# Merge stage: output units as one 512- and one 256-column product, two more copies and sums, another order on ScalarE, and six stores at the end

## The reference, cut to what matters

```python
mixed = (jax.nn.sigmoid(f["g_a"]) * (y_a.astype(dt) @ lp["w_a"])
         + jax.nn.sigmoid(f["g_b"]) * (y_b.astype(dt) @ lp["w_b"]))
return mixed @ lp["w_out"]
...
return _rmsnorm_2(h, final_norm).astype(x.dtype)
```

## Time and profile before

| | |
|---|---|
| median of 3 runs | 2354.12 us (2350.52 to 2354.69) |
| the profiled execution | 2346.09 us |
| its span | 2344.2 us |
| TensorE busy | 2285.3 us, 97% |
| VectorE, ScalarE, GpSimd busy | 1223.2, 1178.7, 1342.1 us |
| merge stage, in the span | about 1000 to 1273 us |
| stores at the end | 4 of 512 KB |

### The profile page before, as it was taken

The page is one execution under the profiler, slowest core; times in us unless marked ns, Lnnn a source line. Parts: engine busy times, 40 slices in busy tenths (PEclk is TensorE's granted clock), DMA queues, the critical chain, the costliest instruction groups (busy, mean ns, idle before and its releaser), DMA issues.

```text
span 2344.2 us, 60261 instructions
## 1 busy us (share of the span) xinstructions
PE 2285.3 (97%) x23364; PEld 1944.4 (83%) x23364; DVE 1223.2 (52%) x2449; ACT 1178.7 (50%) x1999; POOL 1342.1 (57%) x566
## 2 busy tenths in 40 slices
PE   6999999999999999999999999999999999999997
PEld 4787787778777888899999888888888888888886
DVE  2478778877883323466565455453444533333322
ACT  3244545454554444444444555555555555555554
POOL 1112123212332344478888878777777877778785
PEclk8999999999999999999999999999999999999999
DMA  9922112211211223267776555555555555555553
GB/s 389 381 87 66 40 60 77 66 41 58 70 65 50 81 99 108 99 222 251 256 252 244 183 166 176 168 173 173 177 172 171 181 169 172 177 177 172 170 181 134
DMA packets 101244, 360.70 MB, mean 154 GB/s; under 512 B 11184, under 2 KB 14768, under 8 KB 101072
## 3 DMA queue, kind: packets, MB, share of 16 engines
q1 hardware_dynamic: 99872, 356.89, 44.4%
q10 hardware_dynamic: 1200, 1.25, 0.2%
HBM read 356.00 MB, written 2.10 MB: 153 GB/s over the span
## 4 chain that ended last, share of the span: by engine, by line
PE 89%; DVE 2%; ACT 2%; issue 1%; DVEq 0%; ACTq 0%
PE ps L223 32%; PE ps L224 16%; PE ps L684 5%; PE ps L196 4%; PE ps L198 4%; PE ps L197 4%; PE ps L686 4%; PE ps L685 4%; PE ps L815 1%; PE ps L800 1%; PE ps L836 1%; PE ps L980 1%; PE ps L850 1%; PE ps L951 1%; PE ps L1000 1%
## 5 line engine op out<-in xcount | busy, mean ns | idle before, releaser
L187 POOL TENSOR_TENSOR wlo<-raw,whi 128x1024 fp32r<-128x1024 f32 x555 | 1336.7, 2422 | 948.7 <-ACT whi L178 898.7
L223 PE MATMUL ps<-acts,whi 128*128 128x512 f32 x3072 | 1087.6, 398 | 1.3 <-DVE acts L2794 1.3
L224 PE MATMUL ps<-acts,wlo 128*128 128x256 f32 x3072 | 856.7, 279 | 0.0
L178 ACT ACTIVATE whi<-raw 128x1024 fp32r<-128x1024 f32 x562 | 591.6, 1054 | 267.1 <-PE ps L224 138.3
L223 PEld LDWEIGHTS ps<-acts,whi 128*128 128x128 f32 x3072 | 576.2, 188 | 131.6 <-DVE acts L2794 1.6
L224 PEld LDWEIGHTS ps<-acts,wlo 128*128 128x128 f32 x3072 | 579.0, 188 | 0.9
L684 PE MATMUL ps<-acts,whi 128*128 128x512 f32 (+1 forms) x560 | 216.9, 387 | 0.9 <-DVE W L1560 0.9
L686 PE MATMUL ps<-acts,wlo 128*128 128x512 f32 (+1 forms) x560 | 190.1, 339 | 0.0
L685 PE MATMUL ps<-acts,whi 128*128 128x512 f32 (+1 forms) x560 | 189.8, 339 | 0.0
L196 PE MATMUL ps<-acts,whi 128*128 128x256 f32 (+1 forms) x576 | 181.7, 315 | 0.0
L198 PE MATMUL ps<-acts,wlo 128*128 128x256 f32 (+1 forms) x576 | 180.0, 313 | 0.0
(11 more groups left out here) (391 smaller groups left out, 3087.8 us busy)
## 6 DMA issues: line engine op xcount, KB each, us to landing
raw<-stream SPq DMA_DIRECT2D x564, 512.0 KB, 3.3
W<-stream SPq DMA_DIRECT2D x64, 512.0 KB, 9.1
graw<-stream SPq DMA_DIRECT2D x32, 512.0 KB, 4.3
W<-xT SPq DMA_DIRECT2D x4, 1024.0 KB, 8.7
XR<-xT SPq DMA_DIRECT2D x16, 128.0 KB, 5.7
outT<-XR SPq DMA_DIRECT2D x4, 512.0 KB, 3.3
cns<-consts SPq DMA_DIRECT2D x1, 928.0 KB, 11.1
cns<-consts SPq DMA_DIRECT2D x1, 896.0 KB, 7.4
```

Of the source, the lines that this page charges most:

```text
L178: nc.scalar.activation(high, raw[slot], ACT.Copy).then_inc(hi_done, 1)
L187: nc.gpsimd.tensor_tensor(wlo[slot], raw[slot], whi[slot].bitcast(F32), ALU.subtract).then_inc(lo_done, 1)
L223: nc.tensor.matmul(both_parts, whi[slot][:, k, :], hl[:, :, k0 + k, :], start=first and k == 0, stop=False)
L224: ins = nc.tensor.matmul(ps[:, bank, 0:T], wlo[slot][:, k, :], hl[:, 0, k0 + k, :], start=False, stop=last and k == UK - 1)
```

## The change

The output units of a merge tile go through `mm_wide` as well. ScalarE makes two more copies per tile (into `sqv`, free in this stage) and VectorE two more sums, each ahead of the product that reads it. ScalarE's split `hi(k + 7)` moves ahead of the high part of the mixed result. In `out3` the small logarithm that loads the table moves ahead of the last tile's square (for the other output phases its place stays). VectorE's first piece of the last product is cut in two, GpSimd's too, and there are six stores in place of four.

```diff
                     for u in range(2):
                         M["ylo"].wait(pe, (2, 5)[u])
-                        mm_unit(pe, (b + 4 + u) % RING, i * 12 + (b + 4 + u), ps[:, bank + 2 + u, 0:T], 1, UK * u, True,
-                                True)
+                        mm_wide(pe, (b + 4 + u) % RING, i * 12 + (b + 4 + u), bank + 2 + u, acts[:, :, 1], UK * u, True, True)
...
                     hi(k + 5, k + 6)
+                    act.wait_ge(unit_used, i * 12 + (S_MERGE + k + 6))
+                    M["out_sum"].wait(act, i * 4 + 2 * n)
+                    for u in range(2):
+                        parts_copy(act, out_low(u), bank + 2 + u).then_inc(M["out_lo"].sem, 1)
+                    hi(k + 7)
                     M["mix"].wait(act, i * 2 + n + 1)
                     nc.scalar.activation(mhi[:, bass.ds(2 * i + n, 1), :].rearrange("p a t -> p (a t)"), mx[:, n, :],
                                          ACT.Copy).then_inc(M["mhi"].sem, 1)
-                    hi(k + 7)
...
                     for g in range(2):
+                        M["out_lo"].wait(dve, i * 4 + 2 * n + g + 1)
+                        parts_sum(dve, out_low(g), 6 - 4 * n + g).then_inc(M["out_sum"].sem, 1)
+                        M["out_sum"].wait(dve, i * 4 + 2 * n + g + 1)
                         nc.vector.scalar_tensor_tensor(tg[:, n, T * g:T * g + T], tg[:, n, T * g:T * g + T], 1.0,
                                                        ps[:, 6 - 4 * n + g, 0:T], ALU.add, ALU.mult)\
                             .then_inc(M["m1"].sem, 1)
...
                             hi(i, k)
+                        if i == KT // 2 - 1 and k == (4 if base == S_OUT3 else 5):
+                            nc.scalar.activation(small[:, 106:107], kst_[:, 3:4], ACT.Ln if base == S_OUT3 else ACT.Sqrt)
                         if n is not None:
                             tile(i, n)
                         if i == KT // 2 - 1 and k == 5:
-                            nc.scalar.activation(small[:, 106:107], kst_[:, 3:4], ACT.Ln if base == S_OUT3 else ACT.Sqrt)
...
-            for k in range(4, KT, 4):
-                nc.vector.tensor_tensor(XR[:, k:k + 4, :], XR[:, k:k + 4, :],
-                                        ps[:, 7, 0:T].unsqueeze(1).broadcast_to([P, 4, T]), ALU.mult).then_inc(N["x"].sem, 1)
+            for k, n in ((4, 2), (6, 2), (8, 4), (12, 4)):
+                nc.vector.tensor_tensor(XR[:, k:k + n, :], XR[:, k:k + n, :],
+                                        ps[:, 7, 0:T].unsqueeze(1).broadcast_to([P, n, T]), ALU.mult).then_inc(N["x"].sem, 1)
...
-            nc.gpsimd.tensor_tensor(XR[:, 0:4, :], XR[:, 0:4, :], sr[:, T:2 * T].unsqueeze(1).broadcast_to([P, 4, T]),
-                                    ALU.mult).then_inc(N["tab"].sem, 1)
+            for k in (0, 2):
+                nc.gpsimd.tensor_tensor(XR[:, k:k + 2, :], XR[:, k:k + 2, :], sr[:, T:2 * T].unsqueeze(1).broadcast_to([P, 2, T]),
+                                        ALU.mult).then_inc(N["tab"].sem, 1)
...
+            for k, n, ready, value in ((4, 2, "x", 1), (6, 2, "x", 2), (0, 2, "tab", 1), (8, 4, "x", 3), (2, 2, "tab", 2),
+                                       (12, 4, "x", 4)):
+                S["out3"][ready].wait(sp, value)
+                sp.dma_start(outT[:, k:k + n, :], XR[:, k:k + n, :]).then_inc(stored, 16)
+            sp.wait_ge(stored, 96)
```

More of the change, by code:

```diff
@@ L2008, in dve_gla @@
                         .then_inc(G["head_done" if m else "const"].sem, 1)
-        M = counts("m", "yhi ylo x_in c_in tg m1 m2 mix mhi mlo xr gate_in0 gate_in1 gate_acc gate_mm gate_ok gate_lo gate_sum", 1)
+        M = counts("m", "yhi ylo x_in c_in tg m1 m2 mix mhi mlo xr gate_in0 gate_in1 gate_acc gate_mm gate_ok gate_lo gate_sum out_lo out_sum", 1)
         retire(G)
@@ L2045, in gate_low, with out_low @@
             return qk[:, T * g:T * g + T]
+        def out_low(u):
+            return sqv[:, u, 0:T]
         assert M["mix"].base > 1
```

## The result

The changed kernel takes 2380.9 us (median of 6 runs, 2375.8 to 2386.9), the kernel before 2352.6 in the runs beside it: a ratio of 1.0122, 95% interval 1.0109 to 1.0134. It is slower by 28 us. The direction and the place (the merge) were forecast, the size was forecast at 39.

What follows compares the result with a forecast made beforehand. TensorE alone bound the merge before; the change would close a loop of waits of 20.0 us against 17.07 a tile. +41.0, -0.4 in the other two tiles, -1.65 at the end: 2354 + 39 = 2393 us, range 2368 to 2405.

Steps and rivals of the forecast that it cites:

- the loop: Merge: gate products, gate load, unit 3's load and split, copies, sums, mixed result, low part, next gate products; 20.0 us.
- the output copies behind the split of unit 3: Merge, ScalarE: the mixed result waits for copies queued behind a split that waits for DMA, closing the loop.
- Size of a turn: Merge: 5.8 to unit 3's split, 7.8 to the low part's end, 6.4 of gate products: 20.0 us against 17.07.
- When it binds: Merge: slack is used up in the first two tiles, then 14 of 16 run at 20.0 us: +41.0 us.
- The order of the splits: Merge, ScalarE: moving the next split ahead of the high part costs nothing under TensorE, at most 1.06 us in the loop.
- the 7.8: Merge: time in us from the start of unit 3's split to the end of the low part, including holding by GpSimd.
- a loop without holding: Merge: if GpSimd holds none of VectorE's operations, the loop is 17.4 us and the total +3 us.
- Output products: Merge, TensorE: 16 pairs in place of 16 triples save 0.2 us a tile, 3.2 us for 16 tiles.
- The prediction's second sum: Merge, output products: estimate by N/2.4 + 2.5 ns per matmul, 328 against 325 ns, 0.7 us saved in all.
- The end: Output phase: table load ahead of the last square -1.15 us, earlier first store less 0.1 for store costs; -1.65 in all.
- Rivals: Three other merge outcomes: 2349 us (chance 0.14), 2357 us (0.08), 2361 us (0.06).
- The first: Merge: unit 3's load lands in 3.3 us, nothing held, TensorE bounds; gain 4.9 us, time 2349; chance 0.14.

Runs made afterwards that it cites:

- experiment 7: The changed kernel with SyncE's two gate loads one place later in its list, ScalarE's and VectorE's orders kept: ratio to the kernel before 1.0019.
- experiment 4: The changed kernel with the mixed result's high part again ahead of the split of unit 4, copies still behind unit 3's split: ratio to before 1.0023.
- experiment 3: The changed kernel with the two output copies ahead of the splits of units 3 and 4, high part still behind unit 4's: ratio to before 1.0134.
- experiment 2: The kernel before with only ScalarE's split of the next tile's unit 4 moved ahead of the mixed result's high part: ratio to before 1.0120.
- experiment 5: The changed kernel with output copies ahead of the split of unit 3 and high part ahead of the split of unit 4: ratio to before 0.9993.
- experiment 6: The kernel before with the output units as pairs and nothing else, no copies and no sums: ratio to before 1.0005.

## Why the prediction was right, and where it was not

*What bounds, and the loop.* Right in the main. Every link is in the chain of the changed kernel, and shortening the SyncE link (experiment 7) takes away 24 of the 28 us. But the link by which the prediction closes the loop, the output copies behind the split of unit 3, is not the one that matters: with it and without the moved split the loss is 5 us (experiment 4), without it and with the moved split it is 31 (experiment 3).

*Size of a turn, 20.0 against 18.75.* Three terms. From the gate products to the split of unit 3 5.8 was forecast and 5.4 measured, the landing being 4.5 in place of 4.9. From there to the end of the scaling 4.25 was forecast and 4.24 measured, the add held by GpSimd as said. From there to the end of the low part 3.55 was forecast and 2.7 measured: unit 4's load landed 3.0 after unit 3's, not 3.9, so its split was no longer in the high part's way. The prediction had said that an earlier load would leave this sum the same within 0.2; it became 0.8 shorter. Gate products: 6.4 both. Both misses are landing times that were taken from another tile (4.9 and 7.6, here 4.5 and 6.4) with the same loads just ahead in SyncE's list. Why they landed later there was not found; the last older weight load, issued at 1195.5, had landed at 1198.7. 14 x (20.0 - 18.75) = 17.5 us too much, more than the whole miss of 39 against 28: other terms erred the other way.

*When it binds, 14 tiles.* Right: the first turn is 17.2, the next 19.2. 14 turns of 18.96 in place of 17.07 are 26.5 of the merge's 27.3. The turn taken apart above is one of the shorter ones: 14 x 1.68 would be 23.5. What lengthens the others was not separated; in the longest, 19.8, TensorE waits 1.2 for the modulation's gate.

*The order of the splits.* **This step was wrong.** It said that the split ahead costs nothing where TensorE is the bound, and at most 1.06 a tile inside the loop. Experiment 2 shows that it alone makes 1.012, experiment 4 that taking it back recovers 23 us, about 1.7 a tile. What the step missed: the high part thereby waits for a load that stands behind the gate products, and GpSimd is set to work just when the low part needs to get in. The prediction's own terms give more than 1.06: with the high part right behind the scaling at 4.25 and GpSimd idle, the low part ends at 4.25 + 0.81 + 0.42 = 5.5 in place of 7.8. For the same reason its 17.4 for a loop without holding leaves out the split ahead of the high part, which by its own landing gives 18.2. The sum came out near because this cost was inside the 7.8, under the name of the copies. That part is luck: an edit by the prediction's cause, as in experiment 3, would have gained nothing.

*Output products, 3.2 us.* Not there: 0.3 (experiments 5 and 6, merge 265.6 against 265.9). Its rows, 5.75 against 5.59, give 0.16 a tile and 2.6 in all, rounded up to 0.2. The pitch in long stretches, 0.3591 a triple and 0.3467 a pair, gives 3.2. Counting by the pitch of the kernel before was the fault; the pitch itself moves by 2%. The prediction's second sum, 0.7 us, is nearer to the result, but by chance: the Trainium skill (TensorE: Matmul & The Clock Gate, Back-to-back issue gap) calls N/2.4 + 2.5 the gap of an isolated matmul, and no run here has one, since all of these matmuls stand in a stream.

*The end, 1.65.* Table 1.18 against 1.15, stores 0.27 against 0.5. The 0.5 was 0.6 for the earlier first store, less 0.1. The first store is issued 3.66 after TensorE's second sum in place of 5.35, 0.51 sooner beside the table's 1.18; what took half of that back was not taken apart. Both terms are from the trace alone; the times can't tell them from nothing.

*Rivals.* None came about. The first, a TensorE-bound merge, is reached by experiment 5, without its gain of 3.2.

## What to carry to other kernels

Before moving an instruction in an in-order list, write down for each new predecessor what that one waits for, across the queues too: here a split waited for a load, the load stood in SyncE's list behind another load, and that one waited for the very work which the moved instruction feeds. A wait that hurts nobody, as SyncE's 39 us before, is the place to look first, because it shows how much slack a chain has. When an edit moves several instructions, test each move alone on the kernel before and undo each alone on the changed one: here undoing the copies' place showed nothing and undoing the split's place showed nearly all.

## What the runs showed that was not expected

TensorE has two pitches for the same pair of matmuls at the same granted clock (1.00), 0.347 and 0.353 us, within one execution and with the same code. From the merge on each trace has some 50 to 70 changes of pitch, and all of them but at most one fall on a pause. In the output phases, which no experiment changed, both occur in every kernel. The triples have one pitch: 0.359 to 0.360 for three matmuls in every tile, also in experiment 2, where the pairs beside them run at 0.353. Merges with triples after the wide units kept their pairs at 0.347, in both traces that have them without pauses, from the second tile on; with pairs alone the pitch alternated tile by tile (experiments 5 and 6). What chooses it is open. It is worth up to 5 us in a merge of 768 pairs, more than the edit to the products was worth.
